# Eight sample rows of an expert gather, issued between the products of the scatter before it

## What is computed

```python
def hier_moe(h, w_coarse, b_coarse, w_fine, b_fine, w_gate, w_up, w_down):
    t = h.reshape(-1, D)
    ...                       # routing: top-1 group of 4, then top-2 experts of 4 in it
    out = jnp.zeros_like(t)
    for g in range(MOE_GROUPS):
        hid = jax.nn.silu(jnp.einsum('td,edf->tef', t, w_gate[g])) * jnp.einsum('td,edf->tef', t, w_up[g])
        out = out + jnp.einsum('tef,efd->td', hid * comb[:, g, :, None], w_down[g])
    return out.reshape(B, L, D)
```

## Time and profile before

| | us |
|---|---|
| median of 3 runs | 888.24 |
| lowest, highest | 887.42, 891.05 |
| the profiled execution | 891.31 |
| its span, first to last instruction | 889.5 |

### The profile page before, as it was taken

One profiled execution on the slowest core, in us unless ns is written; L12 is line 12 of the kernel. 1 busy time (PEld: TensorE's weight loads), 2 busy tenths in 40 slices (PEclk: granted clock), 3 DMA queues, 4 the chain that ended last, 5 costly groups with the idle time before them and its releaser, 6 DMA issues.

```text
span 889.5 us, 22406 instructions
## 1 busy us (share of the span) xinstructions
PE 785.1 (88%) x9194; PEld 468.5 (53%) x9195; DVE 407.5 (46%) x1085; ACT 279.9 (31%) x562; POOL 128.2 (14%) x214
## 2 busy tenths in 40 slices
PE   3799998999899999996978679976999979989984
PEld 2478886685545544442433458743545434545443
DVE  1158989515544444442423541363444434434444
ACT  2145673403323333232221350141333322323223
POOL 0251778000001010010000000000101000100101
PEclk9999997999999999998988979986999999989987
DMA  9997554778945889999999998495599999999201
GB/s 317 382 252 290 190 177 142 277 261 327 416 204 210 356 308 427 421 424 421 423 416 407 363 388 323 157 371 230 232 374 424 421 423 419 425 419 425 119 1 49
DMA packets 63885, 280.47 MB, mean 315 GB/s; under 512 B 3013, under 2 KB 3627, under 8 KB 55638
## 3 DMA queue, kind: packets, MB, share of 16 engines
q1 hardware_dynamic: 60738, 271.74, 77.7%
q0 software_dynamic: 2432, 6.94, 2.5%
q10 hardware_dynamic: 676, 1.24, 0.5%
HBM read 277.47 MB, written 3.37 MB: 316 GB/s over the span
## 4 chain that ended last, share of the span: by engine, by line
PE 66%; DMA 22%; DVE 4%; ACT 2%; SPq 2%; issue 2%; POOL 0%; POOLq 0%; DVEq 0%; ACTq 0%
PE bank L663 17%; DMA ring<-in_w_up 13%; PE bank L673 7%; PE bank L921 6%; PE bank L784 6%; PE bank L685 6%; PE bank L635 6%; DMA ring<-in_w_in_even 4%; PE bank L530 4%; DMA big<-in_w_up 3%; DMA ring<-in_w_ada 2%; PE bank L578 2%; DVE t L1261 2%; PE bank L643 1%; PE bank L570 1%
## 5 line engine op out<-in xcount | busy, mean ns | idle before, releaser
L1678 DVE SCALAR_TENSOR_TENSOR x<-bank,ada,x 128x256 f32<-128x256 f32 x392 | 162.0, 475 | 0.0
L663 PE MATMUL bank<-ring,big 128*32 128x256 f32 x2112 | 135.2, 399 | 28.9 <-DMA ring<-in_w_up 22.7
L1675 DVE TENSOR_TENSOR big<-big,bank 128x32 f32<-128x32 f32 x98 | 18.4, 188 | 263.7 <-PE bank L685 263.7
L663 PEld LDWEIGHTS bank<-ring,big 128*32 128x32 f32 x2112 | 65.9, 113 | 88.5 <-issue 34.2
L1830 POOL TENSOR_TENSOR big<-t 128x192 f32<-128x192 f32 x51 | 26.5, 519 | 590.8 <-PE bank L635 425.0
L635 PE MATMUL bank<-htm,big 128*32 128x256 f32 (+1 forms) x1224 | 83.5, 386 | 4.8 <-POOL big L1833 4.8
L685 PE MATMUL bank<-big 32*128 32x264 f32 x816 | 77.7, 451 | 4.9 <-DVE x L1261 3.9
L663 PE MATMUL bank<-big 128*32 128x256 f32 x1024 | 65.8, 400 | 10.4 <-issue 5.3
L784 PE MATMUL bank<-big,ring 128*128 128x264 f32 x320 | 74.1, 389 | 0.7 <-DMA ring<-in_w_in_even 0.7
L1196 ACT ACTIVATE big<-bank 128x128 f32<-128x128 f32 x49 | 13.6, 278 | 186.8 <-PE bank L663 186.8
L784 PEld LDWEIGHTS bank<-big,ring 128*128 128x128 f32 x320 | 59.9, 190 | 12.6 <-issue 1.9
(11 more groups left out here) (240 smaller groups left out, 875.9 us busy)
## 6 DMA issues: line engine op xcount, KB each, us to landing
ring<-in_w_ada SPq DMA_DIRECT2D x24, 2048.0 KB, 16.4
ring<-in_w_gate SPq DMA_DIRECT2D x21, 2048.0 KB, 20.0
ring<-in_w_up SPq DMA_DIRECT2D x21, 2048.0 KB, 24.5
ring<-in_w_down SPq DMA_DIRECT2D x21, 2048.0 KB, 25.6
big<-in_w_gate SPq DMA_DIRECT2D x11, 2048.0 KB, 14.0
big<-in_w_up SPq DMA_DIRECT2D x11, 2048.0 KB, 18.5
big<-in_w_down SPq DMA_DIRECT2D x11, 2048.0 KB, 19.6
ring<-in_w_in_even SPq DMA_DIRECT2D x5, 2048.0 KB, 31.4
```

Source lines behind the costliest of these rows:

```text
L663: last = mm(GU[C * q:C * (q + 1), :].rearrange("p (a n) -> p a n", a=2), hgc[:, P * (k % 2) + C * (k // 2):P * (k % 2) + C * (k // 2 + 1)] ...
L1675: v.tensor_tensor(sacc[:, b], sacc[:, b], banks[:, 4:8, SEQ:T], ALU.add)
L1678: last = v.scalar_tensor_tensor(out=x[:, i, 0:SEQ], in0=bank[4 + dq][:, 0:SEQ], scalar=gate[:, i, 0:1], in1=x[:, i, 0:SEQ], op0=ALU.mult, ...
```

## The change

The gather is split into `gather_samples(q)`, one product of the 8 sample rows for the column group q, and `gather_prompt()`, the eight products of the two prompt tiles. The sample products come first (they now start the accumulation) and the prompt tiles close it. For the first chunk both stand one behind the other. In the loop the four sample products of the next chunk stand between the four products of `scatter(0)`, one behind each, and the order of the scatter's quarters becomes 1, 2, 3, 0, in both scatters. The wait for `picked` moves from the gather to the front of `scatter(0)`; the scatter's signal stays with its last product, now that of quarter 0. After the second half of `gate_up` only the prompt tiles remain.

```diff
-                def gather(n):
-
-                    pe.wait_ge(m["picked"], n)
-                    for t in range(TT):
-                        k = min(P, T - t * P)
+                def gather_samples(q):
+
+                    mm(GATH[C * q:C * (q + 1), :], pk[0:NS, 2, :], htm[0:NS, 2, 2 * P * q:2 * P * (q + 1)],
+                       start=True, stop=False, tile_position=(0, C * q))
+
+                def gather_prompt():
+
+                    for t in range(2):
                         for q in range(4):
-                            last = mm(GATH[C * q:C * (q + 1), :], pk[0:k, t, :], htm[0:k, t, 2 * P * q:2 * P * (q + 1)],
-                                      start=(t == 0), stop=(t == TT - 1), tile_position=(0, C * q))
+                            last = mm(GATH[C * q:C * (q + 1), :], pk[:, t, :], htm[:, t, 2 * P * q:2 * P * (q + 1)],
+                                      start=False, stop=(t == 1), tile_position=(0, C * q))
                     last.then_inc(m["gathered"], 1)
...
-                def scatter(b, n):
+                def scatter(b, n, samples=False):
 
                     pe.wait_ge(m["added_" + "ab"[b]], n)
                     if b:
                         pe.wait_ge(m["added_a"], pe.snap(n + 1))
-                    for dq in range(4):
+                    for i, dq in enumerate((1, 2, 3, 0)):
                         r = slice(C * dq, C * (dq + 1))
                         last = mm(bank[4 + dq][:, 0:T], ysb[r, P * b:P * (b + 1)], sct[r, :], start=True, stop=True,
                                   tile_position=(C * dq, 0))
+                        if samples:
+                            gather_samples(i)
                     last.then_inc(m["scattered_" + "ab"[b]], 1)
 
                 pe.wait_ge(E("tm_a"), 2 * TT * (l + 1))
-                gather(1)
+                pe.wait_ge(m["picked"], 1)
+                for q in range(4):
+                    gather_samples(q)
+                gather_prompt()
...
                         pe.wait_ge(m["scat_ready"], g1)
-                        scatter(0, g1)
+                        pe.wait_ge(m["picked"], g2)
+                        scatter(0, g1, samples=True)
                         gate_up(wgu, range(4, KD)).then_inc(m["gu_done"], 1)
-                        gather(g2)
+                        gather_prompt()
```

## The result

| | us |
|---|---|
| before, median of 4 runs | 889.6 |
| changed, median of 4 runs (1134.9 to 1139.6) | 1136.9 |
| ratio, 95% interval | 1.278 (1.274 to 1.283) |
| span of the changed kernel's profiled execution | 1137.7 |

The change costs 247 us. The forecast was 1026 us with a range of 888 to 1045: the direction was right, the size was not. The time lies above the range, and above the 1109 us of rival 1. In the changed kernel the scatter is line L688, the sample products L631, `gate_up` L666, the prompt products L638, the transpose of `hid` L724 and `down` L676.

A forecast was written before the change was run, and what follows sets the result against it. PE was taken to bound about 29 of 49 loop passes, weight loads the rest. Drains of 4.06 less 0.45 gather gain gave 3.6 us per pass, 176.4, less 38.4 of waiting: 138 more, 1026 us, range 888 to 1045.

The forecast's parts named there:

- rival 1: In the expert loops, drains plus half clock over 3.4 us of each pass: 83 us more, 1109 us; chance 0.12.
- What bounds the kernel: In the expert loops PE sets the time, 8.83 us per pass, except in stretches that wait for weight loads.
- the waiting for weights: PE's waits for expert weight loads, 26.4 us in layer 0 and 12.0 in layer 1; all 38.4 given back.
- A change of shape drains, also between free tiles: In the scatter round nothing of the eight products overlaps: 4.72 us, 4.06 more than before.
- The second S: The second 32 by 128 scatter product of the round, which follows the first sample product.
- rivals 2 to 4: Partial to full overlap of scatter and sample products on free tiles: 925, 906, 886 or 894 us; chances 0.12, 0.11, 0.15.
- the sign that the prediction named: Forecast is wrong if the second scatter product starts within 0.1 us of the first.
- The gather's gain: The gather after `gate_up` loses its sample round: 0.45 us per pass, between 0.36 and 0.51, limited by DVE's `hid`.
- The wait for `picked`: Moved ahead of the scatter, which starts over 3.5 us after POOL ends the picks: costs 0.
- the later `scattered_a`: Signal to DVE comes about 3.5 us later, but DVE still has time for its 1.8 us of sums: costs 0.
- The clock: Forecast, chance 0.50, lets PE keep 2.4 GHz; a 128 by 20 tile at a time had kept it.
- The sum: Over 49 passes, 3.6 us each makes 176.4, less 38.4 of waiting: 138 us more.

The follow-up runs named there:

- the pairs: Changed kernel with scatter and sample products alternating two by two, four changes of shape in place of eight: 927.1 us, ratio 1.042.
- the added products of the scatter's shape: Kernel before, plus four unused 32 by 128 products on constants between those of scatter a: 938.5 us, ratio 1.055.
- six changes: Changed kernel with two scatter and two sample products alternating singly, then two scatter together, then two sample together: 1030.0 us, ratio 1.159.
- undrained products: Kernel before, plus eight unused products of the scatter's 32 by 128 shape, two at each place between those of scatter a: 1091.6 us, ratio 1.227.
- split version: Changed kernel with eight `gate_up` products between the second sample product and the third scatter product: 1221.4 us, ratio 1.379.

## Why the prediction was wrong

**What bounds the kernel: right.** Once PE's pass grew, the waiting for weights went; the DMA share in the loops fell from 0.89 and 0.82 to 0.65 and 0.54.

**A change of shape drains, also between free tiles: right, and the size too.** It was taken from changes between overlapping tiles, since no row had free ones. Forecast 0.64 and 0.54 per lone product and 4.72 for the round, measured 0.64, 0.54 and 4.73. The second S starts 1.18 us after the first (338.94 against 337.76), which rules out rivals 2 to 4 by the sign that the prediction named; the pairs (2.39 against 2.40) bear out the price, and the added products of the scatter's shape, which do run side by side, rule out that interleaving as such is slow. The rule cited from the Trainium skill (TensorEngine Tiling, Key Properties), that changing the tiling mode drains the engine, agrees with the 0.64 and 0.54 us, in a case that the trace of before did not contain.

**The gather's gain: right.** Forecast 0.45, measured 0.46, with the transpose waiting for DVE. The wait for `picked` and the later `scattered_a` cost nothing that can be seen.

**The clock: the step that failed.** The forecast let PE keep 2.4 GHz, at 0.50 against 0.12 for rival 1, on the strength of the earlier trace rows: one tile of 128 by 20 had kept the clock. But the same group showed it fall with PE busy 3.40 of 3.40 us behind small products, and the stretch I was about to create had small products that were drained as well. The row that resembled it more was given less weight. In the profile after, each of the 47 passes has the low clock for 3.4 us or more. The sum put this term at nothing; it is about 101 us of the 111 by which the time exceeds the forecast.

**The size of rival 1: too small as well.** It had 3.4 us at half clock per pass, 1.7 us each, 83 in all. In 31 of the 47 steps between the `down` groups that is nearly what is seen: 14.05 us, 1.6 over the 12.44 of the drains (8.83 + 3.61). But in the other 16 the clock is low for 6.8 us, and such passes take 15.5 to 16.9. Together the clock is low for 215 us, 63 stretches of 3.4. The price of one, 1.6 us, comes from the runs with six changes and with undrained products, where passes with and without it stand side by side. Then the sum closes: 47 x 3.6 = 169, less 38 of waiting for weights, plus 63 x 1.6 = 101, is 232, and the loops between these marks grew by 231.6 (341.5 and 355.2 us against 235.3 and 229.7 in the earlier trace rows). The 31 us of low clock that the loops of before had lie within the 38. Of the other 17 us, 15 are in the first pass of each layer (from the first `gate_up` product to the first `down` 6.8 and 8.5 us more), which pays the drains as well, at a mean granted clock of 0.67 and 0.56 against 0.80 and 0.73 before. The last one or two us stay open: 3 more ahead of the experts of layer 0, nearly all of it before the first gather, where nothing was changed, less some 2 elsewhere.

**The range.** It ended at 1045 because rival 1, with its chance of 0.12, was left outside. A rival whose mechanism is in the trace, with a price that could only add to the forecast, belonged inside it. Even so a range up to rival 1's 1109 would have ended below the 1137 measured.

## What to carry to other kernels

Put products of one tile shape together, and count each change of shape as a drain even if the tiles are free: in this kernel 0.09 us (0.31 from the last pass of one shape to the next, less the 0.22 between passes of one shape) and the weight load that is no longer hidden, and above all the loss of whatever ran side by side; a product widened to its neighbours' shape with zero rows can be the cheaper one. Before spreading small products out, ask what the granted clock did behind the lightest stretch of the trace: here the dense work behind them paid 1.6 us and more per pass, on top of the drains. And breaking up a light stretch does not protect the clock by itself.

## What the runs showed of the hardware that I had not expected

- With PE busy without a gap, the granted clock fell to 0.50 in every pass with 4.7 us of lone drained products (in it or behind it), behind 3.56 us (the last 1.2 in pairs) in 26 of 47, behind 2.3 us of lone ones in 30 of 47 of the split version, and behind 2.39 us in pairs in one of 47, which had waited for weights.
- It fell too behind 3.9 us of undrained products of 32 by 128, for the most part one at a time, in 33 of 47 passes.
- Where light work ran at the low clock, the clock stayed low for longer: 10.15 us at 0.50 in the split version, against 3.4 in most passes of the changed one, and 6.8 in the changed one where the fall came early in the round.
- A low stretch of 3.4 us cost 1.6 us of time with PE busy throughout.
- A round of sample products of 128 rows costs 0.43 us (1.29 / 3), the round of 8 rows 0.57 (1.43 less two of 0.43), and the 0.14 between them is the change of shape: the number of rows of a product made no difference to its passes that can be seen.
